# Three of four column panels of the values and gates stage multiplied by Strassen's scheme

## The chip, the core and the metric

The kernel runs on one core of a Trainium2 chip. The metric is the device time of one execution in microseconds (us). The reported time is the median of several executions. TensorE (PE) multiplies, and its weight loads are shown as PEld. VectorE is DVE, ScalarE is ACT, GpSimd is POOL, and SyncE (SP) issues the transfers.

## The reference

The program is a two-layer decoder trunk on 1024 tokens of width 1024: a gated DeltaNet layer and then a forgetting-attention layer (FoX). Each ends in a layer norm and a gated embedding. The change touches one matrix product of the second layer, columns 2048 to 4095 of `x @ w_in`: the values `v` and the gates `z`.

```python
def fox_mixer(x, w_in, b_f, q_norm_g, k_norm_g, w_out):
    h = x @ w_in                                     # x: 1024 x 1024
    q, k, v, z, f_raw = jnp.split(h, [FOX_W, 2 * FOX_W, 3 * FOX_W, 4 * FOX_W], axis=-1)   # FOX_W = 1024
    ...
    log_f = jax.nn.log_sigmoid(f_raw.astype(F32) + b_f.astype(F32))
    c = jnp.cumsum(log_f, axis=1)
    o = forgetting_attention(q, k, v, c)
    o = o * jax.nn.silu(z.reshape(B, S, FOX_HEADS, FOX_DH).astype(F32))
    return o.reshape(B, S, FOX_W).astype(x.dtype) @ w_out
```

## The kernel before

The program is a row of phases with a barrier of all engines between them (line 49). Every large product is made in a split form of float32: an operand is stored as a high part (fp32r, made by ACT) and a low part (the remainder, made by DVE), and a block of the product is the sum of three matmuls, high by high, high by low and low by high. The low by low product is left out.

`fox_values` is the phase "fv". Its tokens come in already split and turned, as `xh` and `xl` (tiles `part_hi`, `part_lo`), 8 blocks of 128 rows by 1024 tokens each. Its work is four column panels of 512 columns. Panels 0 and 1 are the values: the token block is the stationary operand, the weights stream through, and each of 8 banks of PSUM takes one block of 128 tokens by 512 columns. Panels 2 and 3 are the gates: here the weights are the stationary operand and 512 tokens stream through, so the result lies turned. Each panel is 8 tiles, each tile sums over 8 blocks of 128 in three matmuls (L1553 to L1555 for values, L1558 to L1560 for gates). A panel is 192 matmuls of 512 columns, the stage is 768.

SP loads the weights in pieces of 128 rows by 512 columns into a ring of four (`w_raw`). The first four are loaded by the phase before (`ahead`). ACT makes the high part of each piece (`high`, L1624), DVE the low part (`low`, L1661). The split weights lie in two buffers of a whole panel each, so panel n+2 is split while panel n+1 is multiplied. ACT takes the finished banks: a copy for the values (L1636), a Silu for the gates (L1639).

Between the tiles PE also makes the small product for the forget gate `f_raw` (48 matmuls, L1581 to L1583), eight small turns (L1589), the running sums (L1600, L1601) and one more turn (L1605). Their elementwise work is ACT's and DVE's: a bias and an absolute value (L1671, L1672), an exponential (L1649), a logarithm by a series (L138 to L145, called by L1674's `log_one_plus`), and the block totals (L1681 to L1685).

Each engine executes its own program in order. `Step` sets a semaphore behind every instruction and waits for it before the next. SP, at the end, starts the loads of the attention phase (`after.start`) once the last weights are split, and stores the gate sums.

Of the kernel before, what the change touches and what calls it, by code (L numbers as in the profile page):

```python
# [6 lines left out]
F32 = mybir.dt.float32  # L7
F32R = mybir.dt.float32r
# [1492 lines left out]
def fox_values(nc, c, ring, ahead, after, xh, xl, w_in, b_f, c_rows, values, gate_z):  # L1501

    with Phase(nc, "fv") as ph:
        sb, ps, sem = ph.sb, ph.ps, ph.sem
        RAW, PANELS = 4, 4
        w_raw = half_rows(ring)
        w_hi, w_lo = sb("w_hi", [P, 2, KT, HALF], F32R), sb("w_lo", [P, 2, KT, HALF], F32R)
        f_raw, f_hi, f_lo = (sb("f_raw", [P, KT, FH]), sb("f_hi", [P, KT, FH], F32R), sb("f_lo", [P, KT, FH], F32R))
        bias = sb("bias", [P, FH])
        work = [sb(f"work{n}", [P, NT, FH]) for n in range(5)]  # L1510
        rows = sb("rows", [P, P])
        f_rows = gate_z[0:FH, NT - 1]
        bank = [ps(f"bank{n}", [P, HALF]) for n in range(8)]
        w_loaded = [sem(f"w_loaded{n}") for n in range(RAW)]
        small = sem("small")
        act_step, dve_step = sem("act_step"), sem("dve_step")
        w_high, w_low, f_high, f_low = sem("w_high"), sem("w_low"), sem("f_high"), sem("f_low")
        made, taken, f_made, f_log, c_summed, c_ready, c_turned = (
            sem("made"), sem("taken"), sem("f_made"), sem("f_log"), sem("c_summed"), sem("c_ready"), sem("c_turned"))
# [3 lines left out]
        F = NT * FH  # L1523

        @block.sync
        def _(sp):
            sp.dma_start(f_raw[:], w_in[:, 4 * WIDTH:4 * WIDTH + FH].rearrange("(k p) n -> p k n", p=P)
                         ).then_inc(small, 16)
            sp.dma_start(bias[:], b_f.partition_broadcast(P)).then_inc(small, 16)
            for n in range(PANELS):  # L1530
                for k in range(KT):
                    m = n * KT + k
                    if m < RAW:
                        continue
                    sp.wait_ge(w_low, m - RAW + 1)
                    sp.dma_start(w_raw[:, m % RAW], w_in[k * P:(k + 1) * P, 2 * WIDTH + n * HALF:2 * WIDTH + (n + 1) * HALF]
                                 ).then_inc(w_loaded[m % RAW], 16)
            sp.wait_ge(w_low, PANELS * KT)
            after.start(sp)
            sp.wait_ge(rows_made, 1)  # L1540
            sp.dma_start(c_rows, rows[:]).then_inc(stored, 16)
            sp.wait_ge(stored, 16)

        @block.tensor
        def _(pe):
            def multiply(n, t, k):
                b = n % 2
                if k == 0 and n >= 1:

                    pe.wait_ge(taken, (n - 1) * NT + t + 1)  # L1550
                if n < PANELS // 2:
                    ts = slice(t * P, (t + 1) * P)
                    pe.matmul(bank[t][:], xh[:, k, ts], w_hi[:, b, k], start=(k == 0), stop=False)  # L1553
                    pe.matmul(bank[t][:], xh[:, k, ts], w_lo[:, b, k], start=False, stop=False)
                    mm = pe.matmul(bank[t][:], xl[:, k, ts], w_hi[:, b, k], start=False, stop=(k == KT - 1))  # L1555
                else:
                    ch, ts = slice(t // 2 * P, (t // 2 + 1) * P), slice(t % 2 * HALF, (t % 2 + 1) * HALF)
                    pe.matmul(bank[t][:], w_hi[:, b, k, ch], xh[:, k, ts], start=(k == 0), stop=False)  # L1558
                    pe.matmul(bank[t][:], w_hi[:, b, k, ch], xl[:, k, ts], start=False, stop=False)
                    mm = pe.matmul(bank[t][:], w_lo[:, b, k, ch], xh[:, k, ts], start=False, stop=(k == KT - 1))  # L1560
                if k == KT - 1:
                    mm.then_inc(made, 1)

            warm_up(pe, c, bank[NT - 1])
            for k in range(KT):

                pe.wait_ge(w_low, k + 1)
                for t in range(NT):
                    multiply(0, t, k)
            small_bank = bank[NT - 1]  # L1570
            for n in range(1, PANELS):
                pe.wait_ge(w_low, (n + 1) * KT)
                for t in range(NT):
                    if n == 1 and t == 1:

                        pe.wait_ge(taken, NT)
                        pe.wait_ge(f_low, 1)
                        for k in range(KT):
                            for half in range(2):
                                out, ts = bank[NT - 2 + half][0:FH], slice(half * HALF, (half + 1) * HALF)  # L1580
                                pe.matmul(out, f_hi[:, k], xh[:, k, ts], start=(k == 0), stop=False)  # L1581
                                pe.matmul(out, f_hi[:, k], xl[:, k, ts], start=False, stop=False)
                                mm = pe.matmul(out, f_lo[:, k], xh[:, k, ts], start=False, stop=(k == KT - 1))  # L1583
                        mm.then_inc(f_product, 1)
                    if n == 1 and t == 2:

                        pe.wait_ge(f_copied, 2)
                        for i in range(NT):
                            mm = pe.transpose(small_bank[:, i * FH:(i + 1) * FH], f_rows[:, i * P:(i + 1) * P],  # L1589
                                              c["ident"][0:FH, 0:FH])  # L1590
                        mm.then_inc(f_made, 1)
                    if n == 1 and t == NT - 1:

                        pe.wait_ge(abs_made, 1)
                    if n == 2 and t == 1:

                        pe.wait_ge(f_log, 1)
                        pe.wait_ge(taken, 2 * NT)
                        log_f = work[3][:].rearrange("p t h -> p (t h)")
                        pe.matmul(small_bank[:, 0:F], c["tri"][:], log_f, start=True, stop=True)  # L1600
                        mm = pe.matmul(small_bank[:, F:2 * F], c["ones"][:], log_f, start=True, stop=True)  # L1601
                        mm.then_inc(c_summed, 1)
                    if n == 2 and t == 3:
                        pe.wait_ge(c_ready, 1)
                        pe.transpose(small_bank[:, 0:P], work[4][:].rearrange("p t h -> p (t h)"), c["ident"][:]  # L1605
                                     ).then_inc(c_turned, 1)
                    if n == 2 and t == NT - 1:
                        pe.wait_ge(rows_made, 1)
                    for k in range(KT):
                        multiply(n, t, k)  # L1610

        @block.scalar
        def _(act):
            step = Step(act, act_step)

            def high(m):
                n, k = m // KT, m % KT
                if m < RAW:
                    ahead.arrive(act)
                else:  # L1620
                    act.wait_ge(w_loaded[m % RAW], 16 * (m // RAW))
                if n >= 2:
                    act.wait_ge(made, (n - 1) * NT)
                step(act.activation(w_hi[:, n % 2, k], w_raw[:, m % RAW], ACT.Copy), w_high)  # L1624

            for m in range(2 * KT):
                high(m)
            act.wait_ge(small, 32)
            step(act.activation(f_hi[:], f_raw[:], ACT.Copy), f_high)
            for n in range(PANELS):  # L1630
                for t in range(NT):
                    act.wait_ge(made, n * NT + t + 1)
                    half = n % 2
                    cols = slice(half * HALF, (half + 1) * HALF)
                    if n < 2:
                        step(act.activation(values[:, t, cols], bank[t][:], ACT.Copy), taken)  # L1636
                    else:
                        at = slice(t % 2 * HALF, (t % 2 + 1) * HALF)
                        step(act.activation(gate_z[:, (n - 2) * 4 + t // 2, at], bank[t][:], ACT.Silu), taken)  # L1639
                    if n == 2 and t == 4:  # L1640
                        act.wait_ge(c_turned, 1)
                        step(act.activation(rows[:], bank[NT - 1][:, 0:P], ACT.Copy), rows_made)
                if n == 0:
# [5 lines left out]
                    step(act.activation(work[1][:], work[1][:], ACT.Exp), exp_made)  # L1649
# [596 lines left out]
```

## Time and profile before

| what | value |
|---|---|
| time, median of 3 executions | 1758.02 us (1757.87 to 1759.43) |
| the profiled execution: its span | 1755.8 us |
| what lies around the span (median less span) | 2.2 us |
| PE busy | 1687.5 us, 96% of the span |
| weight loads | 1287.9 us, 73% |
| DVE busy | 882.0 us, 50% |
| ACT busy | 788.9 us, 45% |
| the values and gates stage, first to last matmul of the panels | 885.58 to 1073.47 us of the span |

The span is the time from the first to the last instruction of one profiled execution. Busy times of different engines overlap. The start times of two neighbouring matmuls give what one costs in a stream. The duration of one (389 ns here) is longer than that, because it holds the way through the array, in which the next one already streams. An engine's idle time costs something only where another engine waits for it.

### The profile page before, as it was taken

The page shows a single profiled execution, that of the slowest core. Times are in us where ns is not written, and L with a number is a line of the kernel's source. Part 1 is how long each engine was busy: PE and PEld are TensorE (multiplying, and loading weights), DVE is VectorE, ACT ScalarE, POOL GpSimd, SP SyncE. Part 2 cuts the span into 40 slices and gives each one's busy share as a digit, 9 for nine tenths or more (in the row PEclk, how much of TensorE's full clock was granted, in tenths as well). Part 3 has the DMA queues.
Part 4 walks back from the last instruction along what each step waited for, and adds up shares of the span by engine and source line. Part 5 has one row for each costly group of instructions (what it writes and reads, how often), then busy time and mean ns, then how long its engine had stood idle before and what let it go on. Part 6 is the DMA issues. An engine that isn't in the chain of part 4 may idle for free. (4 is left out here: it accounts for less than half of the span.)

```text
span 1755.8 us, 28773 instructions
## 1 busy us (share of the span) xinstructions
PE 1687.5 (96%) x11157; PEld 1287.9 (73%) x11157; DVE 882.0 (50%) x1655; ACT 788.9 (45%) x1288; POOL 312.6 (18%) x243
## 2 busy tenths in 40 slices
PE   9999999999999899799999999999999999899898
PEld 6777777777777677678777887666666665688686
DVE  5757667575666635854322200344444544577533
ACT  4746556464554722142222311556555665531411
POOL 5213212132222251300000000222221221013000
PEclk9999999999999999999989999999999999999999
DMA  6202011210102122051130202111111101051411
GB/s 158 62 26 49 13 50 22 52 37 25 50 13 57 41 97 72 13 168 46 39 110 26 71 2 45 40 45 31 46 35 42 43 22 43 2 175 40 144 46 51
DMA packets 115574, 94.42 MB, mean 54 GB/s; under 512 B 19760, under 2 KB 97776, under 8 KB 115440
## 3 DMA queue, kind: packets, MB, share of 16 engines
q1 hardware_dynamic: 115440, 92.59, 18.5%
q8 instruction: 89, 1.46, 0.3%
q14 instruction: 45, 0.37, 0.1%
HBM read 84.08 MB, written 8.49 MB: 53 GB/s over the span
## 5 line engine op out<-in xcount | busy, mean ns | idle before, releaser
L435 PE MATMUL gdn_unit<-part_hi,gdn_w_hi 128*128 128x512 f32 x496 | 225.7, 455 | 0.0
L437 PE MATMUL gdn_unit<-part_hi,gdn_w_lo 128*128 128x512 f32 x496 | 195.3, 394 | 0.0
L436 PE MATMUL gdn_unit<-part_lo,gdn_w_hi 128*128 128x512 f32 x496 | 194.0, 391 | 0.0
L2108 DVE CUSTOM_DVE_ANT_0 fa_probs<-fa_scores,fa_decay 128x896 f32<-128x896 f32 (+7 forms) x128 | 97.0, 758 | 120.9 <-PE fa_scores L1920 73.6
L867 DVE SCALAR_TENSOR_TENSOR x<-gdn_raw,gdn_taps,x 128x512 f32<-128x512 f32 x144 | 129.4, 899 | 24.3 <-ACT x L665 19.4
L399 POOL TENSOR_TENSOR gdn_w_lo<-ring,gdn_w_hi 128x1024 fp32r<-128x1024 f32 x31 | 75.2, 2427 | 250.7 <-ACT gdn_w_hi L645 250.7
L2054 ACT ACTIVATE fa_probs_t<-fa_turned 128x512 f32<-128x512 f32 (+1 forms) x96 | 52.3, 545 | 139.0 <-PE fa_turned L1937 138.4
L2048 ACT ACTIVATE fa_probs<-fa_probs,fa_top 128x896 f32<-128x896 f32 (+7 forms) x128 | 99.4, 777 | 22.1 <-DVE fa_top L2108 18.4
L437 PEld LDWEIGHTS gdn_unit<-part_hi,gdn_w_lo 128*128 128x128 f32 x496 | 93.1, 188 | 21.0
L435 PEld LDWEIGHTS gdn_unit<-part_hi,gdn_w_hi 128*128 128x128 f32 x496 | 93.7, 189 | 16.1 <-issue 3.6
L1295 PE MATMUL e_gate<-e_w_hi,part_hi 128*128 128x512 f32 x256 | 101.8, 398 | 3.0 <-DVE part_lo L1430 2.8
L436 PEld LDWEIGHTS gdn_unit<-part_lo,gdn_w_hi 128*128 128x128 f32 x496 | 94.1, 190 | 12.1 <-issue 3.6
L1872 PE MATMUL fa_unit<-part_hi,fa_w_hi 128*128 128x512 f32 x224 | 102.1, 456 | 0.0
L1937 PE MATMUL fa_turned<-ident,fa_probs 128*128 128x128 f32 x576 | 96.6, 279 | 3.7 <-ACT fa_probs L2048 2.9
L1297 PE MATMUL e_gate<-e_w_hi,part_lo 128*128 128x512 f32 x256 | 99.9, 390 | 0.0
L1296 PE MATMUL e_gate<-e_w_lo,part_hi 128*128 128x512 f32 x256 | 99.7, 389 | 0.0
L1937 PEld LDWEIGHTS fa_turned<-ident,fa_probs 128*128 128x128 f32 x576 | 68.4, 140 | 40.9 <-issue 15.9
L1874 PE MATMUL fa_unit<-part_hi,fa_w_lo 128*128 128x512 f32 x224 | 88.2, 394 | 0.0
L1873 PE MATMUL fa_unit<-part_lo,fa_w_hi 128*128 128x512 f32 x224 | 87.7, 391 | 0.0
L2115 DVE COPY fa_probs_t<-fa_turned 128x512 f32<-128x512 f32 (+3 forms) x96 | 47.2, 491 | 75.9 <-PE fa_turned L1937 74.7
L1052 PE MATMUL m_y<-part_hi,m_o_hi 128*128 128x512 f32 x200 | 79.9, 399 | 3.9 <-DVE m_o_lo L1128 3.8
L1920 PE MATMUL fa_scores<-fa_qk 64*128 64x512 f32 (+3 forms) x384 | 79.3, 517 | 2.1 <-DVE fa_qk L2148 1.3
(329 smaller groups left out, 3681.0 us busy)
## 6 DMA issues: line engine op xcount, KB each, us to landing
ring<-in_gdn_w_in_dram SPq DMA_DIRECT2D x31, 512.0 KB, 4.1
ring<-in_ple_w_gate_dram SPq DMA_DIRECT2D x32, 256.0 KB, 3.2
ring<-in_fox_w_in_dram SPq DMA_DIRECT2D x32, 256.0 KB, 3.1
ring<-in_fox_w_in_dram SPq DMA_DIRECT2D x16, 512.0 KB, 4.7
fa_decay<-c_rows_scratch SPq DMA_DIRECT2D x64, 128.0 KB, 3.0
gdn_g_bc<-g_rows_scratch SPq DMA_DIRECT2D x8, 512.0 KB, 8.9
x_scratch<-x SPq DMA_DIRECT2D x8, 512.0 KB, 2.9
m_old<-x_scratch SPq DMA_DIRECT2D x8, 512.0 KB, 3.5
```

What stands on the lines that cost most here:

```text
L435: pe.matmul(out, w_hi[:, j % 2, k, :], xh[:, k, ts], start=(k == 0), stop=False)
L436: pe.matmul(out, w_hi[:, j % 2, k, :], xl[:, k, ts], start=False, stop=False)
L437: mm = pe.matmul(out, w_lo[:, j % 2, k, :], xh[:, k, ts], start=False, stop=(k == KT - 1))
L867: step(dve.scalar_tensor_tensor(out, shifted, weight, out, ALU.mult, ALU.add), conv_made if part == TAPS - 1 else None)
L1295: pe.matmul(out[:, cols], hi, w_hi[:, k, cols], start=first, stop=False)
L1296: pe.matmul(out[:, cols], hi, w_lo[:, k, cols], start=False, stop=False)
L1297: mm = pe.matmul(out[:, cols], lo, w_hi[:, k, cols], start=False, stop=end)
L1872: pe.matmul(out, w_hi[:, j % 2, k, :], xh[:, k, ts], start=(k == 0), stop=False)
L1874: mm = pe.matmul(out, w_lo[:, j % 2, k, :], xh[:, k, ts], start=False, stop=(k == KT - 1))
L1937: mm = pe.transpose(turned[by][:, b * P:(b + 1) * P], probs[:, n % 3, j * P:(j + 1) * P], c["ident"][:])
L2048: step(act.activation(own, own, ACT.Exp, bias=top[:, n % 4:n % 4 + 1], scale=-1.0, accum_out=total[:, p % 2, e, head:head + 1]), exped)
L2108: step(dve.tensor_tensor_reduce(probs[:, n % 3, blocks(e)], scores[head][:, blocks(e)], decay[:, head, blocks(e)], 1.0, 3e38, ALU.add, ALU ...
```

## The change

Panel 0 is still multiplied plainly, but in four pieces: two halves of 256 columns by two halves of the sum (`plain`). Panels 1, 2 and 3 are each cut in two by two: two halves of the tokens (512), two halves of the sum (4 blocks of 128) and two halves of the columns (256). Seven products of half size (`wino`, in the order M1, M2, M5, M6, M7, M4, M3) replace the eight. They need four sums of token blocks (`mix_tokens`, made once, split by `high_t` and `low_t`), four sums of weight blocks for each panel (`first_mix`, `next_mixes`, `last_mix`), and sums of results. M2 adds onto M1's bank, M7 and M4 onto M6's, M3 onto M5's. The rest of the sums are made by DVE from PSUM into the results (`add`). Values stream 256 columns of weights (4 tiles for a product), gates stream 512 tokens (2 tiles for a product). The split weights lie in two buffers of one product each (`w_hi[:, g % 2]`), and the raw ones in three. The gates of three of the four quarters get their Silu in a separate pass by ACT (`silu`). The allocation `dynamic_dma_scratch_size=512` makes room in SBUF.

The core of the diff, cut:

```diff
-        RAW, PANELS = 4, 4
-        w_hi, w_lo = sb("w_hi", [P, 2, KT, HALF], F32R), sb("w_lo", [P, 2, KT, HALF], F32R)
+        KH, NW = KT // 2, HALF // 2
+        w_hi, w_lo = sb("w_hi", [P, 2, KH, NW], F32R), sb("w_lo", [P, 2, KH, NW], F32R)
+        t_hi, t_lo = sb("t_hi", [P, 4, KH, HALF], F32R), sb("t_lo", [P, 4, KH, HALF], F32R)
+        extra = sb("extra", [P, KH, NW])
...
+        PLAIN, WINO, PANELS = 4, 7, 4
+        M1, M2, M5, M6, M7, M4, M3 = range(WINO)
+        def tiles(h):
+            return (NT, NT // 2, 2, 2)[h]
...
         def _(sp):
+            for h in range(1, PANELS):
+                sp.wait_ge(w_low, flat(h, M1))
+                load(0, h, 0, 0)
+                sp.wait_ge(w_low, flat(h, M2) + 1)
+                load(1, h, 1, 0)
+                sp.wait_ge(w_low, flat(h, M6) + 1)
+                load(2, h, 1, 1)
+                sp.wait_ge(w_low, flat(h, M7) + 1)
+                load(1, h, 0, 1)
...
         def _(pe):
+            def plain(g):
+                n, k_half = g // 2, g % 2
+                pe.wait_ge(w_low, g + 1)
+                for t in range(NT):
+                    out, ts = bank[t][:, 0:NW], slice(t * P, (t + 1) * P)
+                    for k in range(KH):
...
+            def wino(h, i):
+                g = flat(h, i)
+                pe.wait_ge(w_low, g + 1)
+                fresh = i in (M1, M6, M5)
+                for j in range(tiles(h)):
+                    wait_for_bank(h, i, j)
+                    for k in range(KH):
...
+            def wait_for_bank(h, i, j):
+                elif i == M7:
+                    pe.wait_ge(added, adds + J + j + 1)
+                elif i == M4:
+                    pe.wait_ge(added, adds + 2 * J + j + 1)
...
         def _(act):
+            def high(g):
+                elif i == M5:
+                    act.wait_ge(mixed, 4 * h - 3)
+                else:
+                    act.wait_ge(mixed, 4 * h - 1)
+                if g >= 2:
+                    act.wait_ge(made, made_by(g - 2))
+                step(act.activation(w_hi[:, g % 2], raws[buffer], ACT.Copy), w_high)
...
+            for g in range(PLAIN, PRODUCTS):
+                h, i = at(g)
+                if i in (M1, M2):
+                    if i == M1:
+                        high(g + 1)
+                    take(g)
...
+                if i >= M2 and g + 1 < PRODUCTS:
+                    high(g + 1)
+                if h == 1 and i == M2:
+                    act.wait_ge(abs_made, 1)
+                    step(act.activation(work[1], work[1], ACT.Exp), exp_made)
+                if h >= 2 and i in (M4, M3):
+                    silu(h, M5 if i == M4 else M4)
+                    if i == M3:
+                        silu(h, M3)
...
         def _(dve):
+            for g in range(PLAIN, PRODUCTS):
+                h, i = at(g)
+                if g + 1 < PRODUCTS:
+                    if i == M2:
+                        first_mix(h)
+                    if i == M4:
+                        last_mix(h)
+                    low(g + 1)
+                    if i == M2:
+                        next_mixes()
+                if i >= M5:
+                    add(g)
+                if h == 1 and i == M2:
+                    gate_logs()
+                if h == 1 and i == M6:
+                    gate_log_ends()
+                if h == 2 and i == M1:
+                    gate_totals()
...
-    nc = _bacc.Bacc("TRN2", target_bir_lowering=False, num_devices=1)
+    nc = _bacc.Bacc("TRN2", target_bir_lowering=False, num_devices=1, dynamic_dma_scratch_size=512)
```

`take(g)` copies each tile of product g out of PSUM after that tile is made. The engines' small gate work stays, at other places: PE's small product behind M1 of panel 1, its turns behind M2, the sums and the last turn behind M1 and M2 of panel 2.

## Rows read from the trace of the kernel before

**Rows 1.** The page: engines' busy time over the whole span, and the transfer queues.

```profile
PE 1687.5 (96%) x11157; PEld 1287.9 (73%) x11157; DVE 882.0 (50%) x1655; ACT 788.9 (45%) x1288; POOL 312.6 (18%) x243
q1 hardware_dynamic: 115440, 92.59, 18.5%
```

**Rows 2.** Busy time by stretch: the value panels, the gate panels (granted clock after POOL).

```profile
885.50:985.40 99.90, 99.90 (x442) 77.84 (x441) 19.36 (x37) 23.44 (x39) 0.00 (x0) 0.99 0.20 63
985.40:1073.60 88.20, 88.07 (x391) 72.59 (x389) 7.33 (x17) 16.24 (x27) 0.00 (x0) 1.00 0.09 25
```

**Rows 3.** Timeline of PE: start us, duration us; end of small product, end of stage.

```profile
935.62 0.40 PE L1581 MATMUL fv_bank<-part_hi,fv_f_hi 128*16 128x512 f32 x1
...
946.74 0.39 PE L1553 MATMUL fv_bank<-fv_w_hi,part_hi 128*128 128x512 f32 x1
...
1073.08 0.39 PE L1560 MATMUL fv_bank<-part_hi,fv_w_lo 128*128 128x512 f32 x1
```

**Rows 4.** Timeline of ACT: two takes of neighbouring tiles, the last take.

```profile
1057.24 0.60 ACT L1639 ACTIVATE gate_z<-fv_bank 128x512 f32<-128x512 f32 x1 [4.84 <-PE fv_bank L1560]
1062.68 0.60 ACT L1639 ACTIVATE gate_z<-fv_bank 128x512 f32<-128x512 f32 x1 [4.84 <-PE fv_bank L1560]
...
1073.56 0.60 ACT L1639 ACTIVATE gate_z<-fv_bank 128x512 f32<-128x512 f32 x1 [4.84 <-PE fv_bank L1560]
```

**Rows 5.** A stream of short matmuls, a weight load for each, and their loads.

```profile
595.74 1.95 PE L527 MATMUL gdn_w<-x 128*128 128x128 f32 x16
L527 PEld LDWEIGHTS gdn_w<-x x128: 187/192/192, 69.6 to 597.3; 128*128 128x128 f32 x128
```

**Rows 6.** Groups by shape, DVE: out<-in xcount, busy us, mean ns of one.

```profile
L909 DVE TENSOR_TENSOR o_t<-o_t,x 128x1024 f32<-128x1024 f32 x8 | 9.8, 1226 | 0.3
L2132 DVE TENSOR_TENSOR gate_z<-fa_result,gate_z 128x512 f32<-128x512 f32 x16 | 11.1, 691 | 0.5
L1435 DVE TENSOR_TENSOR e_p_lo<-e_p_tile,e_p_hi 128x256 fp32r<-128x256 f32 x16 | 6.8, 426 | 1.5 <-ACT e_p_hi L1368 1.0
```

**Rows 7.** Groups by shape, ACT.

```profile
L2014 ACT ACTIVATE fa_w_hi<-ring 128x1024 fp32r<-128x1024 f32 x16 | 16.9, 1057 | 0.5
L1106 ACT ACTIVATE part_hi<-ring 128x512 fp32r<-128x512 f32 x16 | 10.1, 632 | 8.3 <-DMA ring<-in_fox_w_out_dram 8.2
L2054 ACT ACTIVATE fa_probs_t<-fa_turned 128x256 f32<-128x256 f32 x8 | 3.1, 384 | 8.8 <-PE fa_turned L1937 8.8
```

**Rows 8.** Timeline of all engines at the attention phase's start: the chain ACT, DVE, PE.

```profile
1076.43 1.06 ACT L2014 ACTIVATE fa_w_hi<-ring 128x1024 fp32r<-128x1024 f32 x1
1077.52 1.23 DVE L2135 TENSOR_TENSOR fa_w_lo<-ring,fa_w_hi 128x1024 fp32r<-128x1024 f32 x1 [76.00 <-ACT fa_w_hi L2014]
...
1078.89 0.47 PE L1872 MATMUL fa_scores<-part_hi,fa_w_hi 128*128 128x512 f32 x1 [1.47 <-DVE fa_w_lo L2135]
```

**Rows 9.** Timeline of DVE: first and last of the gate logarithm's ten instructions.

```profile
954.18 0.23 DVE L138 TENSOR_SCALAR fv_work<-fv_work 128x128 f32<-128x128 f32 x1 [0.51 <-ACT fv_work L1649]
...
958.95 0.29 DVE L1675 SCALAR_TENSOR_TENSOR fv_work<-fv_work 128x128 f32<-128x128 f32 x1
```

**Rows 10.** Transfer issues of the page: count, KB each, median us to landing.

```profile
ring<-in_fox_w_in_dram SPq DMA_DIRECT2D x16, 512.0 KB, 4.7
```

**Rows 11.** Timeline of PE: first matmul after a pause (length in brackets).

```profile
682.02 1.34 PE L123 MATMUL m_y<-tri,ident 128*128 128x128 f32 x8 [2.37 <-PEq L49]
712.87 0.50 PE L1052 MATMUL m_y<-part_hi,m_o_hi 128*128 128x512 f32 x1 [2.26 <-DVE m_o_lo L1128]
1626.73 1.06 PE L1284 MATMUL e_flip<-ident,x 128*128 128x128 f32 x8 [3.40 <-PEq L49]
```

**Rows 12.** Busy time by stretch, behind three of these pauses (granted clock after POOL).

```profile
682.90:686.20 3.30, 3.30 (x11) 2.62 (x10) 1.85 (x4) 2.30 (x4) 0.00 (x0) 0.50 0.88 281
713.60:716.80 3.20, 3.20 (x10) 2.42 (x9) 2.37 (x5) 0.68 (x3) 0.00 (x0) 0.50 0.28 56
1626.80:1631.60 4.80, 2.61 (x19) 2.30 (x20) 4.01 (x7) 4.56 (x8) 0.00 (x0) 1.00 0.58 182
```

More of the change, by code:

```diff
@@ L1525, in _, with parts, load @@
+        def parts():
+            return [slice(0, KH // 2), slice(KH // 2, KH)]
         @block.sync
         def _(sp):
-            sp.dma_start(f_raw[:], w_in[:, 4 * WIDTH:4 * WIDTH + FH].rearrange("(k p) n -> p k n", p=P)
+            def load(buffer, h, n, k):
+                sp.dma_start(raws[buffer], weights(h, n, k)).then_inc(raw_loaded[buffer], 16)
+            load(2, 0, 1, 0)
+            sp.dma_start(f_raw, w_in[:, 4 * WIDTH:4 * WIDTH + FH].rearrange("(k p) n -> p k n", p=P)
                          ).then_inc(small, 16)
-            sp.dma_start(bias[:], b_f.partition_broadcast(P)).then_inc(small, 16)
@@ L1530, in _ @@
[L1530 to L1538, printed above, removed]
+            sp.dma_start(bias, b_f.partition_broadcast(P)).then_inc(small, 16)
@@ L1564, in _ @@
-            warm_up(pe, c, bank[NT - 1])
[L1565 to L1610, printed above, removed]
@@ new lines, in gate_product @@
+            def gate_product():
+                pe.wait_ge(copied, 2 * NT)
+                pe.wait_ge(f_low, 1)
+                for k in range(KT):
+                    for half in range(2):
+                        out, ts = bank[NT - 2 + half][0:FH], slice(half * HALF, (half + 1) * HALF)
+                        pe.matmul(out, f_hi[:, k], xh[:, k, ts], start=(k == 0), stop=False)
+                        pe.matmul(out, f_hi[:, k], xl[:, k, ts], start=False, stop=False)
+                        mm = pe.matmul(out, f_lo[:, k], xh[:, k, ts], start=False, stop=(k == KT - 1))
+                mm.then_inc(f_product, 1)
@@ new lines, in gate_turns, with gate_sums @@
+            def gate_turns():
+                pe.wait_ge(f_copied, 2)
+                for i in range(NT):
+                    mm = pe.transpose(bank[NT - 1][:, i * FH:(i + 1) * FH], f_rows[:, i * P:(i + 1) * P],
+                                      c["ident"][0:FH, 0:FH])
+                mm.then_inc(f_made, 1)
+            def gate_sums():
+                pe.wait_ge(f_log, 1)
+                log_f = logs[:].rearrange("p t h -> p (t h)")
+                pe.matmul(bank[NT - 1][:, 0:F], c["tri"][:], log_f, start=True, stop=True)
+                mm = pe.matmul(bank[NT - 1][:, F:2 * F], c["ones"][:], log_f, start=True, stop=True)
+                mm.then_inc(c_summed, 1)
@@ L1626, in _ @@
-            for m in range(2 * KT):
-                high(m)
-            act.wait_ge(small, 32)
[L1629 to L1643, printed above, removed]
+                elif h == 0:
+                    act.wait_ge(raw_loaded[buffer], 16)
+                elif i == M1:
+                    act.wait_ge(raw_loaded[0], 16 * (h + 1))
+                elif i == M2:
+                    act.wait_ge(raw_loaded[1], 16 * (3 * h - 2))
+                elif i == M4:
+                    act.wait_ge(raw_loaded[2], 16 * (2 * h + 1))
+                elif i == M3:
+                    act.wait_ge(mixed, 4 * h)
+                elif i == M5:
+                    act.wait_ge(mixed, 4 * h - 3)
+                else:
+                    act.wait_ge(mixed, 4 * h - 1)
@@ new lines, in high, with high_t, take @@
+                if g >= 2:
+                    act.wait_ge(made, made_by(g - 2))
+                step(act.activation(w_hi[:, g % 2], raws[buffer], ACT.Copy), w_high)
+            def high_t(n):
+                for part, ks in enumerate(parts()):
+                    act.wait_ge(t_made, 2 * n + part + 1)
+                    step(act.activation(t_hi[:, n, ks], t_raw[n][:, ks], ACT.Copy), t_high)
+            def take(g):
+                h, i = at(g)
+                for j in range(tiles(h)):
+                    act.wait_ge(made, made_by(g) - tiles(h) + j + 1)
+                    if h == 0:
+                        to = values[:, j, g // 2 * NW:(g // 2 + 1) * NW]
+                        step(act.activation(to, bank[j][:, 0:NW], ACT.Copy), copied)
+                    elif i == M1:
+                        step(act.activation(place(h, 1, 0, j), result(h, i, j), ACT.Copy), copied)
+                    else:
+                        step(act.activation(place(h, 0, 0, j), result(h, i, j), ACT.Copy if h < 2 else ACT.Silu), copied)
@@ new lines, in silu @@
+            def silu(h, i):
+                n, t, order = {M5: (1, 1, 3), M4: (1, 0, 4), M3: (0, 1, 5)}[i]
+                for j in range(tiles(h)):
+                    act.wait_ge(added, adds_before(h) + (order - 1) * tiles(h) + j + 1)
+                    step(act.activation(place(h, n, t, j), place(h, n, t, j), ACT.Silu))
+            high(0)
+            high(1)
+            high_t(0)
+            high(2)
+            high_t(1)
+            take(1)
+            high(3)
+            high_t(2)
@@ L1644, in _ @@
+            high_t(3)
+            act.wait_ge(small, 32)
+            step(act.activation(f_hi[:], f_raw, ACT.Copy), f_high)
+            high(4)
+            take(3)
+            for g in range(PLAIN, PRODUCTS):
+                h, i = at(g)
+                if i in (M1, M2):
+                    if i == M1:
+                        high(g + 1)
+                    take(g)
+                if h == 1 and i == M1:
                     act.wait_ge(f_product, 1)
@@ new lines, in low_t, with add @@
+            def low_t(n):
+                for part, ks in enumerate(parts()):
+                    dve.wait_ge(t_high, 2 * n + part + 1)
+                    step(dve.tensor_tensor(t_lo[:, n, ks], t_raw[n][:, ks], t_hi[:, n, ks].bitcast(F32),
+                                           ALU.subtract), t_low)
+            def add(g):
+                h, i = at(g)
+                n, t = {M6: (0, 1), M7: (1, 1), M5: (1, 1), M4: (1, 0), M3: (0, 1)}[i]
+                for j in range(tiles(h)):
+                    dve.wait_ge(made, made_by(g) - tiles(h) + j + 1)
+                    if i == M5:
+                        dve.wait_ge(copied, copies_before(h) + j + 1)
+                    to = place(h, n, t, j)
+                    step(dve.tensor_tensor(to, result(h, i, j), place(h, 1, 0, j) if i in (M5, M6) else to, ALU.add), added)
@@ new lines, in gate_totals @@
+            def gate_totals():
+                dve.wait_ge(c_summed, 1)
+                own = bank[NT - 1][:, 0:F].rearrange("p (t h) -> p t h", h=FH)
+                totals = bank[NT - 1][:, F:2 * F].rearrange("p (t h) -> p t h", h=FH)
+                before, c_all = sums[:, 0], sums[:, 1]
+                step(dve.tensor_copy(before, totals))
+                for t in range(1, NT - 1):
+                    step(dve.tensor_tensor(before[:, t], before[:, t], before[:, t - 1], ALU.add))
+                step(dve.tensor_copy(c_all[:, 0], own[:, 0]))
+                step(dve.tensor_tensor(c_all[:, 1:NT], own[:, 1:NT], before[:, 0:NT - 1], ALU.add), c_ready)
```

250 lines of the change are left out of this document (187 added, 63 removed).

## The prediction

> **What bounds the kernel now.** I read the page's busy times first. PE is busy for 96% of the span, DVE for 50% and ACT for 45% [rows 1]. So a change is worth what it does to PE's stream, and DVE has room on average. The busy time by stretch then shows the stage by itself: over its 188 us, from 885.5 to 1073.6, PE is busy without a break at the full clock, while DVE works 26.7 us and ACT 39.7 us [rows 2]. The reader is to see two things there: nothing waits now, and the split of the weights is hidden wholly.
>
> What does one matmul cost? Its duration of 0.39 us is the way through the array, in which others stream too. The takes by ACT give the true price: two neighbouring tiles end 5.44 us apart [rows 4]. A tile is 24 matmuls, so one of 512 columns costs 0.2267 us. The stage's 768 cost 174.1 us. The small gate product is 48 matmuls between 935.62 and 946.74, 11.1 us [rows 3], and stays. What is left of the stage (some 3 us) are the start at the half clock and the small turns, and stays too.
>
> **PE's work.** Panel 0 becomes 4 x 96 = 384 matmuls of 256 columns. Panel 1 becomes 7 products x 4 tiles x 12 = 336 of 256 columns. Panels 2 and 3 become 7 x 2 x 12 = 168 each, of 512 columns. So 384 wide ones (panels 0 and 1) turn into 720 narrow ones, and 384 (panels 2 and 3) into 336. The wide ones save 48 x 0.2267 = 10.9 us. The narrow price isn't in this trace for this type, and it decides half the gain. Half of 0.2267 is 0.1133. If what stands above pure streaming is a fixed 0.013 us (0.2267 less 512 columns at 2.4 GHz, the level of the granted clock 1.00), it is 0.120. Each narrow matmul still needs its own weight load of 128 columns, whose duration is 0.188 us. But 16 short matmuls with 16 such loads took 1.95 us [rows 5]. Less the last one's way through the array (0.39 less 0.227, some 0.16 us) that is 0.112 us for each load and matmul, so loads overlap each other and don't set a floor at 0.188. I take 0.1167, the middle between 0.1133 and 0.120, and as bounds 0.112 (the short stream) and 0.127 (the fixed part doubled). Then 720 x 0.1167 = 84.0 us against 87.0 us: saved 3.0 us (bounds 6.4 saved, 4.4 lost). PE's work falls by 13.9 us in all. The Trainium skill, "TensorE: Matmul & The Clock Gate", section "Back-to-back issue gap", gives 262 cycles for 256 columns, an estimate of 0.109 us, and 518 for 512, or 0.216; for 512 the trace says 0.2267, so by the page alone the narrow ones would save 5.5 us more, and I keep to the rows.
>
> **The work that lies beside it.** The token sums are 20 DVE instructions of 1024 elements and their low parts 8 more, at 1.226 us [rows 6] 34 us in all. They fall into panel 0, where PE has 4 x 11.2 = 45 us. I followed them in order with the low parts of the pieces between them: the last, before panel 1's first weights, ends about 42 us after the stage's start, the weights of M1 at 43, and PE wants them at 46. Cost nothing, with 3 us in hand. ACT's high parts (1.057 us [rows 7]) go beside it. The results' sums are 0.43 us for 256 columns and 0.69 us for 512 [rows 6], at most 1.8 us per product. The smaller descriptor scratch costs nothing: the transfers of this kernel go through the hardware queue [rows 1].
>
> **Where new waits come.** A half product lasts only 48 x 0.1167 = 5.6 us (panel 1) or 24 x 0.2267 = 5.4 us (panels 2, 3), and its weights must go through ACT and DVE in that time. The buffers hold one product ahead, not one panel. The chain from ACT's start to PE's start is 1.06 + 1.23 us and the handovers, 2.46 us from 1076.43 to 1078.89 [rows 8]. So it matters where it starts.
>
> *Third product of each panel (M5).* ACT's program has the take of M2 ahead of the high part of M5's weights. The take ends only after PE's last matmul of M2. From the start of that matmul: 0.39 and 0.07 until ACT sees it, 0.60 for the last tile, then 2.46 and about 0.03, 3.55 us, where the next matmul would have come after 0.23. Lost 3.3 us in panel 3 and 3.2 in panel 2 (a turn falls into the gap). In panel 1 the tile is narrow (0.384 us [rows 7], the duration shorter by 0.11): 3.1 us lost, less some 0.7 us of turns that PE does meanwhile: 2.4. These three are certain from the order of the program; sum 8.9 us. Queued behind: DVE's `next_mixes` (2.5 us), which M6's weights need. They end 8.3 us after M2's last start, and M6 is due at 9.0: just hidden, but 0.25 us late in panel 1, where the bias, the absolute value and ACT's exponential lie between.
>
> *M4 of panel 1.* DVE has `gate_log_ends` behind M6's sums: from 954.18 to 959.24, 5.1 us [rows 9], then the low part of M4's weights (1.23) and the first sum of M7 (0.43), for which M4's first bank waits. They start 0.66 us after M7's begin, so M4 can start 7.6 us after it, where 5.6 was due: 2.0 us lost.
>
> *First product of panels 2 and 3.* Its raw weights go into the buffer that M3's leave, at about 4.5 us into M4. With a landing of 4.7 us [rows 10] and 2.4 us for the chain they are ready 11.7 us after M4's start, where 10.9 to 11.2 were due. I take 0.45 us each, 0.9; bounds 0 (landing in 4 us) and 2.6.
>
> *The end.* Before, ACT's Silu followed the last matmul directly (0.60 us [rows 4]). Now DVE's sum (0.69 and a handover) and a Silu from SBUF (0.63 [rows 7]) follow: 0.8 us later to the barrier.
>
> Sum of the waits: 8.9 + 0.25 + 2.0 + 0.9 + 0.8 = 12.9 us. Bounds 11 and 15.
>
> **The clock.** PE now stands still for 3.2 us twice and for about 2 us twice. Behind pauses of 2.37 and 2.26 us the granted clock was 0.50 for 3.3 us of work, the lower of its two levels. Behind one of 3.40 us it stayed at 1.00 [rows 11, 12]. At half the clock 3.3 us of work lose 1.65 us. I take two falls over four pauses: 3.2 us; bounds 0 and 6.6.
>
> **Sum.** -13.9 + 12.9 + 3.2 = +2.2, and for the slow restart of a stream (0.34 us instead of 0.23 behind each of eight stops, estimated from the longer first duration in rows 11) +0.8: +3.0 us. The span goes from 1755.8 to 1758.8, with the 2.2 us around it 1761.0 us, against the median of 1758.02.
>
> **The rivals.** *Forecast*: waits and falls eat the saved matmuls, -2 to +7 us, 1756 to 1765. Chance 0.57.
>
> *Faster*: the clock stays at 1.00 through the four pauses, as behind the pause of 3.40 us. That is -3.2 us: -0.2. It decides, as "faster by over 0.2%", only with narrow matmuls at 0.112 too: -3.4 more, -3.6 us, 1754.4; so from 0.112 down. For it speaks the short stream [rows 5], against it the two pauses that were followed by a fall. Chance 0.17.
>
> *Narrow matmuls are dear*: 0.127 or more in place of 0.1167, 720 x 0.0103 = +7.4 us: +10.4, 1768.4. For it speaks that no such stream was seen, against it the 0.112. Chance 0.18.
>
> *The weight load isn't hidden under a short matmul*: a floor of its duration, 720 x 0.188 = 135.4 us, 51 us more: 1812. Against it speaks the stream of 0.112 with the same loads. Chance 0.03. The Trainium skill, same page, Part 3, under "What overlaps and what doesn't", says that a weight load overlaps a matmul in flight only when its row group differs, which would expose every load here; the trace disagrees, since 0.2267 us hold a load of 0.188 beside a matmul of 0.213 us streaming.
>
> *Token sums late*: DVE slips by over 3 us in panel 0, and panel 1 starts late; 2 to 5 us on top, 1764. Chance 0.05.
>
> **How the numbers follow.** A measurement of this kernel tells 0.2%, 3.5 us, from no change. Faster by more: the second case and a tail of the first, 0.18. Slower by more: half of the forecast's range lies above 1761.5 (0.22), all of the dear and exposed cases, nearly all of the last: 0.42. Within: 0.40. The range goes from the second case's lower end, 1753, to the dear case's, 1769; likeliest case alone 1756 to 1765.
>
> **What would show it.** Narrow matmuls 0.112 to 0.120 us apart. PE idle for about 3.1 us before M5 of panels 2 and 3, released by DVE's low part, and ACT's last take ahead of the high part. About 2 us before M4 of panel 1. The granted clock 0.50 behind some of these. The last matmul of the stage near 1075.7. Wrong would be the prediction if the narrow ones cost 0.13 and more, if ACT's high part lay before the take, or if the clock fell at every pause.

## The result, and the profile after

The changed kernel takes 1766.79 us (median of 4 executions, 1766.27 to 1768.61) against 1758.47 us of the kernel before. The ratio is 1.0052, with a 95% interval of 1.0038 to 1.0066. It is 8.3 us slower. The forecast was 1761.0 us, with a range of 1753 to 1769 us, and it gave "slower by more than 0.2%" the largest chance, by a little.

The page of the changed kernel, busy times and transfer queue, answers to [rows 1]:

```profile
span 1766.8 us, 29503 instructions
PE 1685.4 (95%) x11445; PEld 1300.0 (74%) x11445; DVE 960.2 (54%) x1728; ACT 805.8 (46%) x1301; POOL 312.5 (18%) x243
```

PE is busy only 2 us less than before, although its matmuls of the stage hold 12.5% less in the last two panels. DVE works 78 us more. The busy time by stretch (values, then gates) answers to [rows 2]:

```profile
889.00:995.00 106.00, 100.65 (x778) 93.56 (x777) 63.54 (x75) 31.16 (x47) 0.00 (x0) 0.98 0.17 50
995.00:1082.70 87.70, 80.85 (x341) 65.42 (x341) 42.37 (x53) 26.01 (x33) 0.00 (x0) 0.96 0.24 67
```

Before, PE had no break in 188 us. Now it stands still for 12 us of 194, and the granted clock is 0.98 and 0.96 in the two stretches, where it was 0.99 and 1.00. PE's timeline shows where. These are all its pauses of over 0.3 us in the stage (in brackets), and the next phase's first work:

```profile
961.23 0.47 PE L1689 MATMUL fv_bank<-fv_w_hi,fv_t_hi 128*128 128x256 f32 x1 [2.35 <-DVE fv_w_lo L1838]
982.01 0.36 PE L1689 MATMUL fv_bank<-fv_w_hi,fv_t_hi 128*128 128x256 f32 x1 [1.74 <-DVE x L1900]
995.03 0.50 PE L1693 MATMUL fv_bank<-part_hi,fv_w_hi 128*128 128x512 f32 x1 [1.28 <-DVE fv_w_lo L1838]
1009.84 0.80 PE L1693 MATMUL fv_bank<-fv_t_hi,fv_w_hi 128*128 128x512 f32 x1 [3.06 <-DVE fv_w_lo L1838]
1040.81 0.50 PE L1693 MATMUL fv_bank<-part_hi,fv_w_hi 128*128 128x512 f32 x1 [0.58 <-DVE fv_w_lo L1838]
1055.15 0.50 PE L1693 MATMUL fv_bank<-fv_t_hi,fv_w_hi 128*128 128x512 f32 x1 [3.16 <-DVE fv_w_lo L1838]
...
1085.25 1.02 PE L123 MATMUL fa_scores<-tri,ident 128*128 128x128 f32 x7 [2.57 <-PEq L49]
```

In order they are M5 of panel 1, M4 of panel 1 (it waits for a sum in `x`, not for weights), M1 of panel 2, M5 of panel 2, M1 of panel 3, M5 of panel 3. The last pause, at the phase's end, was 1.71 us before.

I measure the stage from its warm-up to the next phase's warm-up. Before that was 881.75 to 1075.18, 193.4 us; now it is 885.19 to 1085.25, 200.1 us: 6.6 us more. So of the 11.0 us between the two spans, 4.4 us lie outside of the stage, and most of these are a difference between executions (below, at after_again).

The chain of a stop can be read from two timelines. ACT, then DVE, before M5 of panel 3:

```profile
1052.08 0.60 ACT L1786 ACTIVATE gate_z<-fv_bank 128x512 f32<-128x512 f32 x1 [2.12 <-PE fv_bank L1695]
1052.71 1.06 ACT L1769 ACTIVATE fv_w_hi<-fv_extra 128x1024 fp32r<-128x1024 f32 x1
```

```profile
1053.87 1.23 DVE L1838 TENSOR_TENSOR fv_w_lo<-fv_extra,fv_w_hi 128x1024 fp32r<-128x1024 f32 x1 [2.60 <-ACT fv_w_hi L1769]
```

ACT takes M2's last tile at 1052.08, only then makes the high part, DVE follows, and PE starts at 1055.15. That is the order the prediction read from the program. It isn't the only thing that is late here: `first_mix`, which makes the sum that ACT has to split, ends at 1051.27. So with the take out of the way the high part could have begun 1.4 us earlier, and no more.

```profile
1050.04 1.23 DVE L1847 TENSOR_TENSOR fv_extra<-ring,fv_extra 128x1024 f32<-128x1024 f32 x1 [4.69 <-DMA ring<-in_fox_w_in_dram]
```

ACT sees the last matmul 0.46 us after its start, so M5 was due at 1051.85, and 3.3 us are lost.

### The profile page after: what moved, and what is told of

Same layout as the page of the kernel before. It is cut to its first block and busy times, and to the rows that moved or that the text cites. A ratio compares the mean times of both kernels' runs of the same rounds, so it can differ in the third digit from the quotient of the medians.

```text
span 1766.8 us, 29503 instructions
## 1 busy us (share of the span) xinstructions
PE 1685.4 (95%) x11445; PEld 1300.0 (74%) x11445; DVE 960.2 (54%) x1728; ACT 805.8 (46%) x1301; POOL 312.5 (18%) x243
```

## The experiments

Each is made on the changed kernel where nothing else is said, and timed beside the kernel before. Ratios are against the kernel before.

### early_take: M5's high part ahead of the take of M2

```diff
                 if i in (M1, M2):
-                    if i == M1:
-                        high(g + 1)
+                    high(g + 1)
                     take(g)
...
-                if i >= M2 and g + 1 < PRODUCTS:
+                if i > M2 and g + 1 < PRODUCTS:
                     high(g + 1)
```

> The changed kernel, with ACT's high part of M5's weights ahead of its take of M2's tiles. Theory (the stops before M5 come from the order of ACT's program): the three idle stretches of PE before M5 (2.35, 3.06 and 3.16 us, 3.1 to 3.3 us lost each) go nearly wholly, and with them the two falls of the clock behind them (1.7 and 3.1 us): 9 to 13 us less than the changed kernel, 1753 to 1758 us. Rival (the weights of M5 are late by their own chain, first_mix and the transfer before it): the stops shrink by under 1 us each and the time stays above 1763 us.

1756.16 us, ratio 0.9992 (0.9984 to 1.0001): about 10 us less than the changed kernel, by two lines of ACT's program. PE's timeline at the places of the three M5:

```profile
999.64 0.47 PE L1693 MATMUL fv_bank<-fv_t_hi,fv_w_hi 128*128 128x512 f32 x1 [1.05 <-ACT gate_z L1786]
...
1040.68 0.50 PE L1693 MATMUL fv_bank<-fv_t_hi,fv_w_hi 128*128 128x512 f32 x1 [1.85 <-DVE fv_w_lo L1837]
```

The stop in panel 1 is gone, that in panel 2 is 1.05 us (3.06 before), and the one in panel 3 is still 1.85 us (3.16 before). The time is in the range expected of the theory. But the theory holds wholly only in panel 1. By the starts of PE's matmuls the order of ACT's program was worth 2.4, 2.0 and 1.3 us of the 9.0 us lost before M5, and a fall of the clock is left behind the stop in panel 3. The rival holds the larger part in panel 3. DVE's timeline there gives the next link of the chain:

```profile
1036.93 1.23 DVE L1846 TENSOR_TENSOR fv_extra<-ring,fv_extra 128x1024 f32<-128x1024 f32 x1 [4.75 <-DMA ring<-in_fox_w_in_dram]
```

`first_mix` waited for a transfer that SP issues after M2's low part, and M2's high part came late (1029.79), because ACT made the last four Silus of panel 2 first, two for M4's quarter and two for M3's.

### warm_waits: work for PE in the stops

```diff
                 g = flat(h, i)
+                if i == M5:
+                    if h > 1:
+                        pe.wait_ge(added, adds_before(h))
+                    for _ in range(12 if h > 1 else 8):
+                        pe.matmul(bank[group(h, M6)][:], xh[:, 0, 0:P], xh[:, 0, 0:HALF], start=True, stop=True)
                 pe.wait_ge(w_low, g + 1)
```

> The changed kernel, with 8 (panel 1) or 12 (panels 2 and 3) matmuls of 512 columns on the tokens, whose result nothing reads, issued by PE while it waits for M5's weights. Theory (part of the loss is the lower clock behind the stops): the granted clock stays at 1.00 in the stage, the stops stay as long, and 4 to 5 us go: 1762 to 1763 us. Rival (the clock's part is small, or falls for another reason): within 1 us of the changed kernel, 1766 to 1768 us, or slower by what the additional matmuls delay.

1760.99 us, ratio 1.0023 (1.0013 to 1.0032): 5 to 6 us less than the changed kernel, with more work on PE, and 1 us better than expected. The waits themselves are as long: M5 of panel 2 starts 14.83 us after M1 of that panel, and 14.85 in after_again. The busy time by stretch behind the three M5 starts (the clock stands after POOL), of the changed kernel's second run (after_again) and then of this one:

```profile
959.30:962.50 3.20, 3.20 (x17) 3.20 (x16) 2.07 (x4) 0.90 (x2) 0.00 (x0) 0.50 0.00 0
1007.10:1010.30 3.20, 3.20 (x8) 2.52 (x9) 2.29 (x2) 0.79 (x1) 0.00 (x0) 0.50 0.00 0
1051.50:1054.70 3.20, 3.20 (x9) 2.53 (x8) 2.04 (x2) 1.05 (x1) 0.00 (x0) 0.50 0.00 0
```

```profile
957.60:961.00 3.40, 3.40 (x28) 3.40 (x29) 2.98 (x4) 0.22 (x1) 0.00 (x0) 1.00 0.00 0
1004.80:1008.00 3.20, 3.20 (x15) 2.63 (x16) 2.32 (x2) 0.77 (x1) 0.00 (x0) 1.00 0.02 5
1047.20:1050.40 3.20, 3.20 (x15) 2.60 (x16) 2.29 (x2) 0.79 (x1) 0.00 (x0) 1.00 0.00 0
```

In equal time 8 or 9 wide matmuls went through at 0.50, and 15 at 1.00. The stage takes 196.1 us, 4.9 less than in after_again. So the clock's part of the stage's loss is shown: some 5 us against an execution with three falls.

### narrow_before: the kernel before with the value panels' matmuls cut in two

```diff
-                    pe.matmul(bank[t][:], xh[:, k, ts], w_hi[:, b, k], start=(k == 0), stop=False)
...
+                    for half in range(2):
+                        cs = slice(half * 256, (half + 1) * 256)
+                        out = bank[t][:, cs]
+                        pe.matmul(out, xh[:, k, ts], w_hi[:, b, k, cs], start=(k == 0), stop=False, skip_group_check=True)
...
```

Its value panels lose a part of their sums; every matmul is made.

> The kernel before, with each matmul of the two value panels cut into two of 256 columns: 384 more matmuls and weight loads, the same columns, no other change. Theory (a fixed 0.013 us for each matmul): 0.120 us apart in place of 0.227 for the wide one, +5.1 us, 1763.5 us. Rival 1 (the price goes with the columns, 0.1133 us): no change. Rival 2 (the 0.120 of the changed kernel came from its other work beside it, DVE and ACT on the same memory): under +2 us.

1762.88 us, ratio 1.0032 (1.0021 to 1.0044): +5.1 us, where a fixed part of 0.013 us for 384 more matmuls makes 5.1. The interval spans 3.7 to 7.7 us, so the time excludes both rivals, and the price itself is read from PE's timeline:

```profile
949.77 0.28 PE L1556 MATMUL fv_bank<-fv_w_hi,part_hi 128*128 128x256 f32 x1
949.89 0.28 PE L1557 MATMUL fv_bank<-fv_w_lo,part_hi 128*128 128x256 f32 x1
950.01 0.28 PE L1558 MATMUL fv_bank<-fv_w_hi,part_lo 128*128 128x256 f32 x1
```

They are 0.120 us apart, with none of the changed kernel's other work beside them. Both rivals fall.

### scratch_before: the kernel before with the smaller descriptor scratch

```diff
-    nc = _bacc.Bacc("TRN2", target_bir_lowering=False, num_devices=1)
+    nc = _bacc.Bacc("TRN2", target_bir_lowering=False, num_devices=1, dynamic_dma_scratch_size=512)
```

> The kernel before, with the smaller descriptor scratch of the changed kernel and nothing else. Theory: no effect, within 0.1% of before. Rival: the smaller scratch delays something outside the stage and holds the 3 us by which the changed kernel's profile is later before its stage begins.

1757.89 us, ratio 1.0001 (0.9993 to 1.0010). The scratch costs nothing.

### after_again: the changed kernel once more

> The changed kernel unaltered, once more, on the same chip and in the same rounds as the next three. All theories: 1765 to 1768 us, 1.004 to 1.006 of before; the stage from its first narrow matmul to the next phase's warm-up 6 to 7 us longer than before (189.6 us).

1766.10 us, ratio 1.0044 (1.0031 to 1.0056). This time its stage begins at 881.76, as before (881.75), so the 3.4 us by which the first profile began later belong to that execution and not to the change. The stage takes 201.0 us to 1082.80, 7.6 us more than before, where 6 to 7 was expected. The clock fell behind all three M5 stops this time (the rows above), behind the first two in the first profile.

### split_logs: the gate logarithm in two parts

```diff
                 if h == 1 and i == M6:
-                    gate_log_ends()
+                    gate_log_starts()
+                if h == 1 and i == M4:
+                    gate_log_ends()
```

`gate_log_starts` holds the first five instructions of the logarithm, `gate_log_ends` the series.

> The changed kernel, with the gate logarithm on DVE in two parts: the first five instructions stay behind M6's sums, the series moves behind M4's sums. Theory: the stop of 1.74 us before M4 of panel 1 goes and nothing takes its place: 1.5 to 2 us less than the changed kernel. Rival: the series then delays the weights of panel 2's M1, and the stop there grows from 1.28 us by as much: no change.

1762.43 us, ratio 1.0026 (1.0016 to 1.0036): 3.7 us less than after_again, by the medians. In PE's timeline the pause before M4 of panel 1 is gone, and that before M1 of panel 2 has not grown (0.84 us, after_again 1.23):

```profile
991.10 0.50 PE L1693 MATMUL fv_bank<-part_hi,fv_w_hi 128*128 128x512 f32 x1 [0.84 <-DVE fv_w_lo L1838]
```

The theory holds in place and sign: all nine executions are faster than all five of after_again. The size is above the 1.5 to 2 us expected. This execution had one fall of the clock less in the stage than after_again, which is worth 1.6 us, and whether the missing stop was its cause isn't shown.

### free_buffer: M3's mixed weights in buffer 1

```diff
-            return (0, 1, 2, 0)[i] if h == 0 else (0, 1, 2, 0, 1, 2, 0)[i]
+            return (0, 1, 2, 0)[i] if h == 0 else (0, 1, 2, 0, 1, 2, 1)[i]
...
                     sp.wait_ge(mixed, 4 * h)
-                    load(1, h + 1, 0, 1)
+                    load(0, h + 1, 0, 0)
                     sp.wait_ge(w_low, flat(h, M4) + 1)
                     load(2, h + 1, 1, 1)
+                    sp.wait_ge(w_low, flat(h, M3) + 1)
+                    load(1, h + 1, 0, 1)
...
-                sub(raws[0], raws[1], raws[0])
+                sub(raws[1], raws[1], raws[0])
```

> The changed kernel, with M3's mixed weights in buffer 1 in place of buffer 0, so that the raw weights of the next panel's M1 are issued about 2.5 us earlier and ahead of two others. Theory (they are late by their issue and by the queue before them): the stops before M1 of panels 2 and 3 (1.28 and 0.58 us) go: 1.5 to 2 us less. Rival: M2's raw weights, now issued later, stop PE instead, and nothing is gained.

1764.16 us, ratio 1.0027 (1.0016 to 1.0038): 1.9 us less than after_again, by the medians. The two intervals overlap, so the size is rough. No pause of over 0.3 us stands before M1 of panel 2 or 3 in its trace, and none before M2, where the rival put it. The changed kernel's timelines of SP and ACT show the transfer that was late in panel 2:

```profile
984.53 0.37 SPq L1601 DMA_DIRECT2D ring<-in_fox_w_in_dram  x1
984.94 0.51 SPq L1601 DMA_DIRECT2D fv_extra<-in_fox_w_in_dram  x1
987.00 0.37 SPq L1601 DMA_DIRECT2D ring<-in_fox_w_in_dram  x1
```

```profile
992.59 1.06 ACT L1769 ACTIVATE fv_w_hi<-ring 128x1024 fp32r<-128x1024 f32 x1 [6.95 <-DMA ring<-in_fox_w_in_dram]
```

The third transfer is the urgent one. It was issued at 987.00, 5.0 us after the start of M4, behind two of 512 KB, and was there at 992.5, 5.5 us later. The prediction had taken 4.5 and 4.7. In free_buffer it is issued 2.5 us into M4, first of the three, and is there after 4.1 us. The edit changes the time of issue and the place in the queue together, so it doesn't say which counts more. The queue alone doesn't explain the 5.5 us: in panel 3 the same three issues follow each other at the same distances, and the third (1033.90) was there after 4.4 us. Why panel 2's takes longer is open.

### all_four, and its second run

The three edits of early_take, split_logs and free_buffer together, and one more:

```diff
+                    if h == 3 and i == M1:
+                        silu(2, M3)
                     take(g)
...
-                    if i == M3:
+                    if i == M3 and h == PANELS - 1:
                         silu(h, M3)
```

> The changed kernel with the three rearrangements (M5's high part first, logarithm in two parts, M3 in buffer 1) and one more: ACT makes M2's high part of panel 3 ahead of the Silu of panel 2's M3, which in early_take delayed the chain to M5 (a stop of 1.85 us). Theory (the loss is in the waits and the clock behind them, the narrow matmuls cost 2.4 us more than forecast): all stops under 0.5 us, no fall of the clock in the stage, 12 to 14 us less than the changed kernel, 1752 to 1755 us, 4 to 6 us faster than before. Rival (DVE or ACT is by then the bound of the stage): stops of over 1 us remain at other products, and the time stays within 0.2% of before.

1749.77 us, ratio 0.9953 (0.9941 to 0.9966). That is 8.2 us less than the kernel before and 16.3 us less than after_again, where 12 to 14 us were expected. The stops were expected to stay under 0.5 us. One pause of over 0.3 us is left in the stage, and the clock doesn't fall in it:

```profile
996.84 0.47 PE L1695 MATMUL fv_bank<-fv_t_hi,fv_w_hi 128*128 128x512 f32 x1 [1.05 <-ACT gate_z L1788]
...
1064.97 2.25 PE L123 MATMUL fa_scores<-tri,ident 128*128 128x128 f32 x18 [2.57 <-PEq L49]
```

The stage is 881.13 to 1064.97, 183.8 us, 9.6 us less than before. The sum of the terms says nearly the same: 11.5 us of matmuls saved, less 1.2 for the stop and 0.9 at the end, makes 9.4. So 0.2 us of the stage are left unexplained. The stop before M5 of panel 3 is gone here, but the fourth edit was not run by itself, so its share isn't shown.

> The kernel of all_four unaltered, beside early_table. All theories: 1749 to 1751 us, 0.994 to 0.997 of before.

1748.69 us, ratio 0.9946 (0.9932 to 0.9960), just under the 1749 to 1751 us expected.

### early_table: the table for Silu loaded while ACT waits

```diff
+                    if h == 2 and i == M2:
+                        nc.scalar.preload_act_table_set("silu_and_others")
                     high(g + 1)
```

> The kernel of all_four, with ACT's table for Silu loaded before the high part of M5's weights of panel 2, while ACT waits for the mixed weights. Theory (the last stop, 1.05 us before M5 of panel 2, is the load of 1.28 us ahead of two takes): the stop goes and 1 us with it, 1748 to 1749 us; no stop of over 0.3 us is left in the stage. Rival (the stop is the takes themselves): no change.

1748.03 us, ratio 0.9946 (0.9933 to 0.9958), timed together with all_four_again. PE's and ACT's timelines:

```profile
998.32 0.50 PE L1695 MATMUL fv_bank<-fv_t_hi,fv_w_hi 128*128 128x512 f32 x1 [0.33 <-DVE fv_w_lo L1843]
```

```profile
992.69 1.28 ACT L1813 ACT_TABLE_LOAD   x1
995.87 1.06 ACT L1771 ACTIVATE fv_w_hi<-fv_extra 128x1024 fp32r<-128x1024 f32 x1 [1.90 <-DVE fv_extra L1852]
```

In all_four the same load stood behind the high part, at 994.81, and the two takes followed it. The pause fell from 1.05 to 0.33 us, so the theory holds in the trace for most of the stop. The medians differ by 0.7 us, which the two intervals can't tell from nothing.

## Why the prediction was right, and where it was short

The mechanism was right in the main: PE's stream saves 11.5 us, and waits that weren't there before, with the clock behind them, take more than that back. The sign and the range held. The size was short: +3.0 us was forecast and +8.3 measured, 1.8 us above the likeliest case's own range of 1756 to 1765 us. Three terms of the sum were too small: the narrow matmuls by 2.4 us, the first products by 1.3 and the clock by 1.2. The range held by some luck, since its upper end, 1769, came from the case in which narrow matmuls cost 0.127 us, and they cost 0.120. By its own steps:

- *PE's work, -13.9 us*: measured -11.5. This was the largest mis-sized term. The price of a narrow matmul was 0.1167, taken from the middle, and 0.120 was measured. 720 x 0.0033 is 2.4 us. The prediction had named the fixed part as one end, and narrow_before shows it is the right one. Panels 0 and 1 together now cost 86.4 us of matmuls against 87.0: Strassen's scheme saves 3.2 us on panel 1, and the cutting of panel 0 takes 2.6 of them.
- *The token sums in panel 0, nothing*: right, no pause over 0.3 us lies there.
- *M5's stops, 8.9 us*: measured 2.4 (3.1 less the turns), 3.3 and 3.3, 9.0 us. The size came out, but "certain from the order of the program" holds for 5.7 us of it: early_take leaves 1.2 us in panel 2 and 2.0 in panel 3. In panel 2 most of the rest is the table load for Silu (early_table), which the prediction didn't have. In panel 3 it is the late `first_mix`, which would have cost some 2 us in any order of the take. That the sum of 8.9 was met so closely is in part luck.
- *M6 of panel 1, 0.25 us*: no pause over 0.3 us.
- *M4 of panel 1, 2.0 us*: measured 1.9, and the sum of M7 as the releaser, as forecast. Shown by split_logs.
- *First products of panels 2 and 3, 0.9 us*: measured 1.4 and 0.8, 2.2 us. In panel 3 the lateness is that of the prediction's own chain, 11.7 us where 10.9 was due. In panel 2 both the issue (5.0 us into M4) and the landing (5.5 us) came later than it had taken. That M1's raw weights are the cause is shown by free_buffer.
- *The end, 0.8 us*: measured 0.9. From the last matmul's start to the next warm-up 2.96 us (1082.29 to 1085.25), before 2.10 [rows 3, and 1075.18].
- *The clock, two falls and 3.2 us*: two falls in the first profile, one of them 6.8 us long (1009.2 to 1016.0), some 4.4 us in all; three in after_again, some 4.7 us. So the count of two was right for one execution, and the length was short. warm_waits, with no fall in the stage, is 5 to 6 us faster. The prediction's comparison was weaker than it looked: the pause of 3.40 us behind which the clock "stayed" was followed by a fall after all (last section).
- *Slow restarts, 0.8 us*: measured about 0.6. Behind the three stops that ended at the high clock the second wide matmul starts 0.33 to 0.34 us after the first.

These sum to -11.5 + 9.0 + 1.9 + 2.2 + 0.9 + 4.4 + 0.6 = +7.5 us, and the stage measured +6.6. The first profile's stage has 4.5 us of low clock at its start, where the kernel before has 5.8, which is worth some 0.6 us. In after_again, where the start is the same as before, the sum is 7.8 and the stage measured +7.6. Of the rest of the time the runs show this much: from the next phase's warm-up to the end of the span both profiles of the changed kernel have 0.9 to 1.0 us more than before. Its code there is the same, and scratch_before, which has none of the change, has 1.0 us more too (1075.67 to 1757.3), with the same longer stretches of low clock. So this part isn't the change's. What sets it wasn't tried.

The rivals: "narrow matmuls are dear" was right in kind, with a third of its price. "The clock stays" was wrong, though which stops are followed by a fall differs from one execution to the next. The late token sums didn't come. The chances don't add up as the prediction says: its own parts for "slower by more" (0.22, 0.18, 0.03 and nearly 0.05) make 0.48 and not 0.42, and what it calls half of the forecast's range is 3.5 of 9 us. An exposed weight load was wrong: narrow matmuls ran 0.120 us apart with loads of 0.188 to 0.192 us. For 256 columns the Trainium skill ("TensorE: Matmul & The Clock Gate", "Back-to-back issue gap") gives 262 cycles, an estimate of 0.109 us; here the trace has 0.120, and the measurement decides.

What wasn't tried: Strassen's scheme on the gate panels alone, with wide matmuls for both value panels. Whether its split weights find room beside the token sums in this layout wasn't worked out. By the rows it would save 10.9 us of matmuls against 11.5, without panel 1's stops.

## What to carry to other kernels

When the work on the bound engine gets shorter in pieces, every chain that feeds a piece has to fit into the shorter piece: write down, for each piece, what the feeding engines do before it in their own order. Here two lines of ScalarE's order were worth 10 us, against the 11.5 us of matmuls that the whole scheme saves, and with four such moves the same algorithm went from 0.5% slower to 0.5% faster. When one chain is late, work out when the next one behind it would have been ready: moving the take gave back 1.3 us of the 3.3 us in panel 3, because the sum before it was late too. Count stops on TensorE at more than their length, since the lower clock behind them cost some 4.5 us here on top of 13.1 us of stops, and count a fixed price for each matmul before halving its columns.

## What the runs showed of the hardware that was not expected

The fixed part of 0.013 us per matmul of this type is there only at the high clock. At 1.00 the starts are 0.227 us (512 columns) and 0.120 us (256) apart. At 0.50 they are 0.427 and 0.214 us apart, 512 and 256 columns at 1.2 GHz with nothing on top. PE's timeline of the changed kernel behind two stops:

```profile
961.50 0.42 PE L1690 MATMUL fv_bank<-fv_w_lo,fv_t_hi 128*128 128x256 f32 x1
961.72 0.42 PE L1691 MATMUL fv_bank<-fv_w_hi,fv_t_lo 128*128 128x256 f32 x1
961.94 0.41 PE L1689 MATMUL fv_bank<-fv_w_hi,fv_t_hi 128*128 128x256 f32 x1
...
1010.43 0.63 PE L1694 MATMUL fv_bank<-fv_t_lo,fv_w_hi 128*128 128x512 f32 x1
1010.86 0.63 PE L1695 MATMUL fv_bank<-fv_t_hi,fv_w_lo 128*128 128x512 f32 x1
```

Stops shorter than the 3.40 us of [rows 11] were followed by a fall: the one of 2.35 us with short turns ahead of it in all four profiles that had it (the first, after_again, split_logs, free_buffer), the one of 3.06 us in the same four, the one of 1.85 us in early_take. The one of 3.16 us was followed by a fall in one of these four. And the pause of 3.40 us isn't a case of a clock that stays. The window in [rows 12] ends at 1631.60, and the fall begins right behind it, 5 us after PE went on and after one more pause of 2.19 us. PE's timeline of the kernel before:

```profile
1631.40 0.39 PE L1297 MATMUL e_proj<-e_w_hi,e_p_lo 128*128 128x512 f32 x1
1631.62 0.55 PE L1295 MATMUL e_proj<-e_w_hi,e_p_hi 128*128 128x512 f32 x1
1631.97 0.63 PE L1296 MATMUL e_proj<-e_w_lo,e_p_hi 128*128 128x512 f32 x1
1632.39 0.63 PE L1297 MATMUL e_proj<-e_w_hi,e_p_lo 128*128 128x512 f32 x1
```

From 1631.97 on the starts are 0.43 us apart. In after_again the same pause, also 3.40 us long, had the low clock before it was over: the first work behind it, at 1635.94, ran at 0.50. So the length of a stop alone doesn't tell in these traces whether a fall follows.
